# Modulation products in packs of twelve, decay attention with four heads interleaved, softmax attention in head pairs

## The reference, cut to what matters

```
mx = split(silu(c) @ w_mod[l] + b_mod[l], 9)           # modulation, 9 x 1024 values, two rows (c, c_ctx)
x, z = x + 0.5*mx[2]*swiglu(modulate(rms(x))), the same for z        # FFN 1
hx, hz = modulate(rms(x)) @ w_in[l], modulate(rms(z)) @ w_in[l]
mix = concat(fourier_mix, neighborhood_attention, bidir_gla, gqa)    # token mixing, 4 heads each
x = x + mx[5]*(mix_x @ w_out[l]);  FFN 2                             # in layer 0 for z too

# gla, both directions, 4 heads, dk = 32, dv = 64:
S_t = diag(exp(a_t)) S_{t-1} + k_t^T v_t;   o_t = q_t S_t            # first over z, its state starts x
o = rms(o_f + o_b) * gain * silu(r)
# attention (gqa over x and z keys; na over a window of x with a bias, and z; in layer 0 also for z's queries)
p = softmax(q k^T [+ bias]);  o = p v                                # head size 64
```

## Time and profile before

| | us |
|---|---|
| median of 3 runs (3769.97 to 3772.39) | 3770.73 |
| the profiled execution's own time | 3772.5 |
| its span, first to last instruction | 3770.6 |
| token mixing, layer 0, from GLA's first product to the output projection | 2117.7 to 2319.4 |
| the same, layer 1, from the end of the last projection | 3370.5 to 3500.9 |
| mean granted TensorE clock | 0.96 of full speed |

### The profile page before, as it was taken

One profiled execution on the slowest core, in us unless ns is written; L12 is line 12 of the kernel. 1 busy time (PEld: TensorE's weight loads), 2 busy tenths in 40 slices (PEclk: granted clock), 3 DMA queues, 4 the chain that ended last, 5 costly groups with the idle time before them and its releaser, 6 DMA issues.

```text
span 3770.6 us, 41915 instructions
## 1 busy us (share of the span) xinstructions
PE 3586.9 (95%) x16488; PEld 2889.8 (77%) x16488; DVE 1675.7 (44%) x3447; ACT 601.8 (16%) x1266; POOL 42.8 (1%) x44
## 2 busy tenths in 40 slices
PE   7999999999999999799999889999989999889999
PEld 6888888888888888688874554688878888455788
DVE  4567223145672231465544443564656555415100
ACT  2121112111211120100013123100010000312100
POOL 0000000000000000000000010000000000001000
PEclk9999999999999999899999769999999999996999
DMA  4777547537775575232322110232323233211354
GB/s 155 201 198 231 171 150 201 156 107 204 199 224 167 153 205 155 69 107 73 88 65 73 34 12 23 67 106 63 97 59 90 90 89 86 62 56 12 101 159 120
DMA packets 656961, 440.69 MB, mean 117 GB/s; under 512 B 25600, under 2 KB 655872, under 8 KB 656640
## 3 DMA queue, kind: packets, MB, share of 16 engines
q1 hardware_dynamic: 652416, 430.28, 39.4%
q0 software_dynamic: 1296, 3.15, 0.8%
q10 hardware_dynamic: 3056, 4.59, 0.3%
HBM read 436.93 MB, written 1.05 MB: 116 GB/s over the span
## 4 chain that ended last, share of the span: by engine, by line
PE 93%; DVE 3%; ACT 2%; issue 1%; ACTq 0%; DMA 0%; POOL 0%; DVEq 0%; POOLq 0%
PE psum L1636 46%; PE psum L1810 22%; PE psum L1833 11%; PE psum L1643 2%; PE psum L1759 2%; PE psum L1907 2%; PE psum L1988 1%; PE psum L1777 1%; PE psum L1767 1%; PE psum L1963 1%; PE psum L1977 1%; PE psum L1922 1%; DVE arena L1404 0%; PE psum L1653 0%; PE psum L1926 0%
## 5 line engine op out<-in xcount | busy, mean ns | idle before, releaser
L1636 PE MATMUL psum<-hh,ring 128*128 128x256 f32 (+1 forms) x5600 | 1367.8, 403 | 37.9 <-ACT hh L1048 19.3
L1636 PEld LDWEIGHTS psum<-hh,ring 128*128 128x128 f32 x5600 | 1063.2, 191 | 300.2 <-issue 162.4
L1636 PE MATMUL psum<-arena,ring 128*128 128x256 f32 x1568 | 341.8, 381 | 8.2 <-DVE arena L1381 5.5
L1636 PEld LDWEIGHTS psum<-arena,ring 128*128 128x128 f32 x1568 | 298.7, 191 | 51.0 <-DVE arena L1381 6.3
L1810 PE MATMUL psum<-hh,ring 128*128 128x256 f32 x1056 | 246.9, 388 | 20.4 <-ACT hh L1048 20.4
L1810 PE MATMUL psum<-hh,arena 128*128 128x256 f32 x1056 | 254.4, 384 | 8.1 <-issue 8.1
L1810 PEld LDWEIGHTS psum<-hh,ring 128*128 128x128 f32 x1056 | 205.5, 195 | 52.8 <-issue 22.8
L1810 PE MATMUL psum<-arena 128*128 128x256 f32 x1056 | 238.7, 379 | 0.0
L1296 DVE SCALAR_TENSOR_TENSOR arena<-arena,par 128x255 f32<-128x255 f32 (+14 forms) x480 | 225.2, 469 | 17.0
L1810 PEld LDWEIGHTS psum<-hh,arena 128*128 128x128 f32 x1056 | 203.7, 193 | 37.5 <-issue 9.2
L1833 PE MATMUL psum<-arena 128*128 128x256 f32 x1056 | 231.8, 379 | 0.0
(11 more groups left out here) (248 smaller groups left out, 3130.0 us busy)
## 6 DMA issues: line engine op xcount, KB each, us to landing
ring<-in_ffn_w SPq DMA_DIRECT2D x176, 512.0 KB, 5.1
ring<-in_w_mod SPq DMA_DIRECT2D x72, 1024.0 KB, 7.5
ring<-in_w_in SPq DMA_DIRECT2D x54, 1024.0 KB, 5.3
ring<-in_w_up SPq DMA_DIRECT2D x88, 512.0 KB, 5.3
ring<-in_w_in SPq DMA_DIRECT2D x84, 512.0 KB, 5.3
ring<-in_w_down SPq DMA_DIRECT2D x16, 1408.0 KB, 7.0
ring<-in_ffn_w SPq DMA_DIRECT2D x12, 1536.0 KB, 6.6
ring<-in_ffn_w SPq DMA_DIRECT2D x12, 1280.0 KB, 5.9
```

What stands on the lines that cost most here:

```text
L1636: ins = mm(o[0:rows_, 0:T], w[:, k, c0:c0 + rows_], src[:, k, 0:T], start=(k == 0), stop=(k == kt - 1))
```

## The change

It does four things. **Packs:** up to twelve consecutive `mod` products accumulate in one fixed bank (bank 7), each shifted to its own pair of rows by taking silu(c) at another offset of a zero-padded buffer; `mod_t` comes once per pack (three per layer), with 24 columns per matmul, and ACT copies the bank at the `mod_t` step. While the first block runs, ordinary jobs rotate over 7 banks. The first `mod` of a pack waits for that copy of the pack ahead.

```diff
     if c < NMOD * KT // 2:
         p.step("mod", l, c)
-        p.job("mod", l, c, chunk=("mod", l, c))
-    if c:
-        p.step("mod_t", l, c - 1)
-        p.job("mod_t", l, c - 1)
+        p.chunks.append(("mod", l, c))
+        p.last_mod[("mod", l, c)] = len(p.last_mod) + 1
+    if c and c % PACK == 0 or c == NMOD * KT // 2:
+        p.step("mod_t", l, (c - 1) // PACK)
+        p.job("mod_t", l, (c - 1) // PACK)
...
+                    if first and packs(l, i // PACK) > 1:
+                        pe.wait_ge(mod_moved, packs(l, i // PACK) - 1)
```

```diff
-                    if lp == 0:
-                        free(tt(four_blocks(gacc), src, mask, ALU.mult), j)
-                    else:
-                        free(tt(four_blocks(gtmp), src, mask, ALU.mult), j)
-                        do(tt(gacc, gacc, gtmp, ALU.add))
-                    if lp == GLA_LEVELS // 2 - 1:
-                        g3 = four_blocks(gacc)
-                        do(tt(at_m[:, hd, 0:4:3, :], g3[:, 0], g3[:, 1], ALU.add), level_added, lev(l, s, hd))
+                    for hd in range(4):
+                        j = job[("g_lv", l, s, hd, lp)]
+                        src = bank(j).rearrange("p (v t c) -> p v t c", v=2, t=TT)
+                        dst = at_m[:, hd, 0:4:3, :]
+                        produced(dve, j)
+                        do(nc.vector.copy_predicated(dst, mask[:, 2 * lp].to_broadcast([P, TT, P]), src[:, 0]))
+                        free(nc.vector.copy_predicated(dst, mask[:, 2 * lp + 1].to_broadcast([P, TT, P]), src[:, 1]), j)
```

On TensorE the heads' loop is now the innermost:

```diff
-                    ph = slice(32 * hd, 32 * hd + 32)
...
+                            for twice in range(2 if diag else 1):
+                                for hd in range(4):
+                                    ph = slice(32 * hd, 32 * hd + 32)
...
+                                    ins = mm(o[hd][:, c0:c0 + P], *kq, start=(twice == 0), stop=(twice == 1 or not diag))
```

```diff
+            for i in range(2):
+                p.step("gp", l, i)
+                p.job("gp", l, i, chunk=("w2", l, "glaqk"))
         if 1 <= n <= len(order):
...
+        if n == 4:
+            p.step("g_exp", l, 1)
+        if n == 6 and last:
+            p.step("g_exp", l, 0)
```

```diff
     units = mix_units(last)
-    p.step("na_load", l)
     for n in range(len(units) + 4):
-        if n == len(units) - 8:
-            p.step("na_bias", l)
-            for hd in range(4):
-                p.job("flip", l, hd)
         if n < len(units):
             p.step("at", l, n)
-            p.job("at", l, n)
+            for b in range(2):
+                p.job("at", l, n, b)
+        if n == 0:
+            gla_norm(0)
         if 1 <= n <= len(units):
             p.step("at_n", l, n - 1)
+        if n in (2, 3):
+            for hd in (2 * n - 4, 2 * n - 3):
+                p.step("na_bias", l, hd)
+                p.job("flip", l, hd)
...
-                    do(nc.vector.reduce_max(stat[:, 6:7], bank(j)[:, 0:nk], AX_X))
-                    do(ts(stat[:, n % 2:n % 2 + 1], stat[:, 6:7], -1.0, None, ALU.mult), max2_ready, n + 1)
...
+                        do(nc.vector.reduce_max(stat2[:, i:i + 1], bank(j)[:, 0:nk], AX_X, negate=True), max2_ready, 2 * m + b + 1)
```

More of the change, by code:

```diff
@@ L45 @@
 BANKS = 8
+PACK = 12
 BANK = 512
@@ L164, in __init__ @@
         self.parts = {}
+        self.ring = BANKS - 1
+        self.last_mod = {}
+        self.next_bank = 0
+        self.uses = [0] * BANKS
+        self.place = []
     def step(self, kind, l, *a):
@@ L170, in job @@
         self.number[name] = len(self.number)
+        b = self.next_bank % self.ring
+        self.place.append((b, self.uses[b]))
+        self.uses[b] += 1
+        self.next_bank = b + 1
         if chunk is not None:
@@ L331, in mix_units @@
     groups = [("gqa", 0)] + ([] if last else [("gqa", 1), ("na", 1)]) + [("na", 0)]
-    return [(kind, s, h, t) for kind, s in groups for h in range(4) for t in range(TT)]
+    heads = {"gqa": ((0, 3), (1, 2)), "na": ((0, 1), (2, 3))}
+    return [(kind, s, hds, t) for kind, s in groups for hds in heads[kind] for t in range(TT)]
 def plan_second(p, l):
@@ L393, in plan_second, with gla_scores, gla_out @@
         p.job("gv", l, t, chunk=("w2", l, "glav"))
[L394 to L412, removed]
-        else:
[L414 to L418, removed]
-                for g in range(2):
-                    p.step("four2", l, s2, g)
-                    p.job("four2", l, s2, g)
+    p.step("g_kt", l)
+    p.job("g_kt", l)
+    for d in range(2):
+        p.step("g_s0", l, d)
+        p.job("g_s0", l, d)
+    def gla_scores(s):
+        p.step("g_x", l, s)
         for hd in range(4):
-            p.step("g_x", l, s, hd)
             p.job("g_x", l, s, hd)
-            for lp in range(GLA_LEVELS // 2):
-                p.step("g_lv", l, s, hd, lp)
+        for lp in range(GLA_LEVELS // 2):
+            p.step("g_lv", l, s, lp)
+            for hd in range(4):
                 p.job("g_lv", l, s, hd, lp)
+    def gla_out(s):
         for pr in range(2):
@@ L760, in ffn_at, with packs, mod_count @@
             return 2 * l + w
+        n_packs = -(-NMOD * KT // 2 // PACK)
+        mod_t_jobs = [None] + [job[("mod_t", l, i)] for l in range(DEPTH) for i in range(n_packs)]
+        def packs(l, i):
+            return n_packs * l + i + 1
+        def mod_count(l, i):
+            return plan.last_mod[("mod", l, min(PACK * (i + 1), NMOD * KT // 2) - 1)]
         def unit_before(hd, t, d):
@@ L1173, in _ @@
+                    for b in range(2):
+                        act.wait_ge(max2_ready, 2 * m + b + 1)
+                        i = 2 * (m % 2) + b
+                        do(nc.scalar.activation(p2[:, n % 4, b, 0:nk], bank(job[("at", l, n, b)])[:, 0:nk], ACT.Exp,
+                                                bias=stat2[:, i:i + 1], accum_out=stat2[:, 4 + i:5 + i]),
+                           exp2_done, 2 * m + b + 1)
                 elif kind == "at_t":
-                    u = mix_units(l == DEPTH - 1)[r[0]]
+                    n = r[0]
@@ L1180, in _ @@
+                    for b in range(2):
+                        j = job[("at_t", l, n, b)]
+                        produced(act, j)
+                        free(nc.scalar.activation(pt2[:, n // 2 % 2, b, 0:nt, u[3] * P:(u[3] + 1) * P],
+                                                  bank(j)[:, 0:nt * P].rearrange("p (k t) -> p k t", k=nt), ACT.Copy), j)
                 elif kind == "at_o":
-                    u = mix_units(l == DEPTH - 1)[r[0]]
+                    u = mix_units(l == DEPTH - 1)[2 * r[0]]
@@ L1893, in _ @@
-                    done(ins)
+                        for hd in range(4):
+                            ph = slice(32 * hd, 32 * hd + 32)
+                            ins = mm(o[hd][:, d * P:(d + 1) * P], expo[ph, 8, d * P:(d + 1) * P],
+                                     expo[ph, 0, (1 - d) * P:(2 - d) * P], start=True, stop=True)
+                            if d:
+                                done(ins)
                 elif kind == "g_lv":
-                    s, hd, lp = r
-                    o = begin(job[("g_lv", l, s, hd, lp)])
```

398 lines of the change are left out of this document (237 added, 161 removed).

## The result

The changed kernel takes **3630.6 us** (median of 4 runs, 3626.8 to 3634.8) against 3770.9 of before: ratio **0.963**, 95% interval 0.961 to 0.964. The forecast was 3621, range 3586 to 3672. Its profiled execution has a span of 3631.2 us.

What follows compares the result with a forecast made beforehand. The prediction took TensorE, busy 95% of the span, as the bound. Terms −23 − 33 − 4 − 3 − 11 − 17 − 63 = −154, less low clock behind the product stages −149.5, gave 3621 us, range 3586 to 3672.

Steps and rivals of the forecast that it cites:

- Packs: First block: 66 `mod_t` go at 0.44 us each, six stay with 1.0 us of handover each: −23 us, bounds −12 and −29.
- Products: Decay attention's three product stages: four row groups at once, VectorE's masked copies become the limit, 74.8 to 42 us: −33.
- Context's `g_o` and `g_n`: Layer 0's token mixing: 7.5 us shrink by interleaving and cover to 3.5: −4 us.
- Waits: Token mixing: old idle goes, new waits come behind `g_exp`: net −3 us in layer 0, −11 in layer 1.
- Trims: Layer 1: five projections over 256 instead of 512 columns, 3.45 us each: −17 us.
- Attention with `g_o`: Softmax attention and `g_o` of x: −34 us in layer 0, −29 in layer 1, −63 together; bounds −89 and −33.
- busy for 80% of these stretches: Sign for attention in both layers: VectorE, not TensorE, would be busy for 80% of it.
- Low clock through attention: Rival: TensorE stays at 1.2 GHz through attention, and weight loads are paced: 3670 us, chance 0.15.
- Matmuls not concurrent: Rival: matmuls of different row groups run one after the other, a stage 34 us instead of 14: 3716 us, chance 0.05.
- Copies at 0.69 or dearer: Rivals on product stages: predicated copies at 0.69 us, 3639, chance 0.12; expensive copies, deciding from 2.3 us, 3853, chance 0.02.
- better case: Rival: stages at 11 us (−9), attention units 0.3 shorter (−7), entries 5 shorter (−10): 3595 us, chance 0.08.
- the rule weighed in the prediction: Product stages: 128-column weight loads may take 0.105 to 0.115 us however few rows: 17 to 18.4 us a stage, +10.

Runs made afterwards that it cites:

- serial_out: Changed kernel with `at_o` of a head pair one head after the other instead of alternating between the halves of the output rows: 3635.2 us.
- exp_later: Changed kernel with the context's `g_exp` behind the `gv` projections, Fourier projections ahead of `g_kt`, and layer 1's x `g_exp` behind the states: 3610.9 us.
- wide_layer1: Changed kernel with layer 1's five trimmed projections back at 512 columns: 3651.1 us.
- bank_at_exp: Changed kernel with the bank of a unit's scores given back by ScalarE's exponential instead of VectorE's reciprocal: 3614.4 us.
- norm_in_r: Changed kernel with v projections behind x's products, x's `g_o` and `g_n` between them, normalised outputs written over r's buffer: 3620.9 us.
- serial_heads: Changed kernel with the four heads one after the other, not alternating, inside each step of decay attention's products: 3658.7 us.

## Why the prediction was right, point by point

- **Packs, −23 against −19.0.** Right, mechanism and prices. The waits were 6.5 us where I took 6. TensorE's busy time up to the gate projections fell from 1889.4 to 1864.1, 25.3 for 66 `mod_t` and not 29.0. The missing 4 are clock, which the forecast did not have: in before 52.4 us of this busy time were at half clock, in the changed kernel's execution 61.6, which makes it about 4.6 longer, and without that a `mod_t` is 0.45 us, where I took 0.44. That this half-clock time differs as much between executions of the same first block (45.3 in serial_out) makes it chance, as far as the runs show.
- **Products, −33 against −36.6** (74.8 to 38.2). The masked copy was the largest unknown and the bounds held it: 0.45 us for 256 columns where I took 0.42, far from the 0.69 of a rival and the 2.3 at which all would have been lost. The first of the two copies of each bank, over both stages of layer 0 (busy us, mean ns, idle before):

```profile
L1652 DVE COPY_PREDICATED arena<-consts,psum 128x256 f32<-128x256 int32 x32 | 14.4, 450 | 30.2 <-PE psum L1997 29.2
```

  The stage is shorter than 14 because TensorE may start its last step when VectorE is through the second, the lower end of the forecast (10.1), and that step's 48 instructions take 2.95. The projections behind layer 0's two stages took 14.9 and 15.3 us for 14.1 at full clock, so the low clock behind a stage cost 0.9 and 1.2 where I took 1.5.
- **Context's `g_o` and `g_n`, −4 against −4.7.** They take 1.9 and 0.9 us.
- **Waits.** In layer 0 I followed the queue to 7.4 and 8.6; it is 7.98 and 7.57. In layer 1 8.5, and it is 8.25. This is the part that exp_later confirms by removing it. The bias DMAs on GpSimd's queue, which I cost at nothing, gave TensorE no wait in either layer. What is left of layer 0 when the terms measured by themselves are taken off is −0.2, where −3, and 3 of low clock behind the stages, were forecast; in layer 1 −11.6 against −11 and 1.5.
- **Trims, −17 against −17.1** (wide_layer1).
- **Attention with `g_o`, −63 against −51.2** (−27.8 and −23.4). Here the forecast was 6 us a layer too good, and it is the term that was mis-sized most. I had taken VectorE for the limit of the units and said that it would be busy for 80% of these stretches. It was busy for 59% and 49%, TensorE for 66% and 70%: that sign failed. Neither engine is full, because the units wait for banks. 4.5 jobs go to 8 banks in each unit, so `at_o`, the next scores and every second unit's `at_t` need a bank with scores that were written one or two units before, and only VectorE's reciprocal, behind the next unit's maximum, gave it back. The context's units took 2.9 us where 2.5 was forecast, x's with bias 4.6 where 4.2 was; bank_at_exp shows the cause by taking it away. The entry's two table loads and VectorE's `g_n` I had counted, but not the wait of 9.4 behind them: the flip stood waiting for the first unit's bank. Most of that one is `g_n` in the way: bank_at_exp turns it into a wait of 7.9 for VectorE's multiply, and norm_in_r alone leaves nothing ahead of this flip.
- **Rivals.** Low clock through attention: the granted clock was 0.94 and 0.86; out. It came back later than I had said in layer 1, where the middle third of the stretch was still at 0.82. Matmuls not concurrent: 48 instructions in 2.95 us at half clock; out. Copies at 0.69 or dearer: 0.45; out. Of the better case the stages came by 1.3 us each of its 3, the units and entries went the other way.
- **Bounds.** Two do not follow from the terms beside them: attention without the 0.6 in 22 units, the low clock and the ends is −94 and not −89, and six projections of 3.6 us held up leave −8 of the packs' 29 and not −12. The range does not hang on them. The low-clock terms and the 1.0 us of a handover rested on no row. The handover took 1.1; for the 3 us of low clock a layer behind the `nss` and state waits, exp_later gives 4.6 us of busy time in both layers together.

The sum was 10 us too good of 140, within the range, and its errors partly cancelled: attention +11.8, packs +4, products −3.6, waits about −2. The packs' 4 are the clock of this execution and no term of the sum; that the products and the waits made up for half of what was missing in attention is luck.

## What to carry to other kernels

When small matmuls are interleaved, the stage's time is that of the engine that takes their banks; price that engine first, and count the bank ring in jobs per iteration: the bank should be given back by its last reader, not by a later step of another engine. An early start of a long chain (exponents here) costs what stands behind it on every queue; put it where the projections under it need none of those engines. Prices taken from a stretch where one head runs alone overstate what undoing the interleaving costs, because even blocks of eight instructions a head overlapped at their seams (0.07 us an instruction against 0.111). And before several small gains are added up, look at the scatter of what they are all measured against: it enters the sum once for each.

## What the hardware showed that I had not expected

At a granted clock of 1.00, float32 matmuls of 32 rows, with 128 weight columns and 128 moving ones, started every 0.111 us an instruction where 36 in a row share a row group (before), every 0.07 on average where it changes after eight (serial_heads), and four in 0.112, one for each row group, where it changes with every matmul. A whole step of the last kind, with its start and the length of its last matmul, is 0.037 an instruction:

```profile
2067.60 1.17 PE L1997 MATMUL psum<-arena 32*128 32x128 f32 x32
```

At 0.50 the starts are 0.213 and 0.147 us apart, and four in 0.213 (a step of 48 in 2.95 us). So four row groups ran at once in full, 4.0 times from start to start and 3.0 times with the ends of a step of 32, and the pace of a 128-column weight load, the rule weighed in the prediction, does not bind across row groups. The Trainium skill ("TensorE: Matmul & The Clock Gate", "LDWEIGHTS (loading the stationary operand)") gives the load of P columns as P/1.2 ns, which for 128 is 107 ns as an estimate. The 0.115 of `mod_t`, which moves two columns, agrees. So does the 0.111 of one row group, but it does not show the load's pace by itself: the projections take 7.15/32 = 0.223 us for 256 moving columns and 7.03/16 = 0.439 for 512, and by these 128 would need 0.11 for the moving columns alone. The Trainium skill's 3.07 times for four row tiles ("Part 3") is for 512 moving columns; no run here has four row groups with 512, and with 128 it is the 3.0 and 4.0 above.

The masked copy out of PSUM costs 0.45 us for 256 float32 columns, against 0.69 for a multiply of 512: per column it is dearer, per operation cheap enough to replace a multiply, an addition and their buffers.
